# Attention heads of an encoder layer: one turned block in another PSUM bank, finer waits of the score maps, and two steps placed later

## What is computed

```python
s = q @ k.T * scale - slope * abs(qpos - kpos)     # for each of two query/key maps of 64
p = softmax(s)                                     # in fp32
w = p[map 0] - lam * p[map 1]
o = w @ v                                          # v has 128 columns
att = rms_norm(o, subln_g) * (1 - lam_init)
```

## Time and profile before

| | |
|---|---|
| time, median of 3 runs (lowest, highest) | 2149.84 us (2144.47, 2150.08) |
| the profiled execution: time, span | 2152.86 us, 2150.6 us |
| mean granted clock of TensorE in it | 0.971 |
| attention heads, sample | about 405 to 726 us |
| attention heads, prompt | about 888 to 1030 us |

### The profile page before, as it was taken

The page is one execution under the profiler, slowest core; times in us unless marked ns, Lnnn a source line. Parts: engine busy times, 40 slices in busy tenths (PEclk is TensorE's granted clock), DMA queues, the critical chain, the costliest instruction groups (busy, mean ns, idle before and its releaser), DMA issues. The chain is left out here.

```text
span 2150.6 us, 43727 instructions
## 1 busy us (share of the span) xinstructions
PE 2009.0 (93%) x16136; PEld 1760.4 (82%) x16136; DVE 1439.9 (67%) x2601; ACT 1109.6 (52%) x1983; POOL 361.3 (17%) x587
## 2 busy tenths in 40 slices
PE   7999998899998998888899399999999999999996
PEld 5887876788887776777788399999999999999895
DVE  5366466566776656766268667777777777778776
ACT  5322322466667333465222166666666666667674
POOL 1223223000000223001221101111111111111234
PEclk9999998999999999999899699999999999999998
DMA  5211100100020223212332278888878787888995
GB/s 184 85 31 32 35 27 17 44 16 24 25 65 26 67 59 90 61 49 74 118 118 99 104 255 256 254 253 256 259 249 259 252 259 248 264 270 284 331 327 188
DMA packets 183467, 317.84 MB, mean 148 GB/s; under 512 B 11872, under 2 KB 82016, under 8 KB 183328
## 3 DMA queue, kind: packets, MB, share of 16 engines
q1 hardware_dynamic: 169984, 281.06, 39.2%
q0 software_dynamic: 8608, 30.68, 5.7%
q10 hardware_dynamic: 4736, 4.19, 0.6%
HBM read 279.97 MB, written 35.91 MB: 147 GB/s over the span
## 5 line engine op out<-in xcount | busy, mean ns | idle before, releaser
L2347 DVE TENSOR_TENSOR we_lo<-raw,we_hi 128x1024 fp32r<-128x1024 f32 x384 | 466.0, 1223 | 204.7 <-ACT we_hi L2272 203.8
L2238 PE MATMUL psum<-x_parts,we_hi 128*128 128x384 f32 x2048 | 584.9, 359 | 3.3 <-DVE x_parts L2354 3.3
L2240 PE MATMUL psum<-x_parts,we_lo 128*128 128x192 f32 x2048 | 513.3, 251 | 0.0
L2272 ACT CAST we_hi<-raw 128x1024 fp32r<-128x1024 f32 x384 | 400.1, 1053 | 186.9 <-PE psum L2240 94.9
L2240 PEld LDWEIGHTS psum<-x_parts,we_lo 128*128 128x128 f32 x2048 | 392.0, 191 | 0.6
L2238 PEld LDWEIGHTS psum<-x_parts,we_hi 128*128 128x128 f32 x2048 | 385.2, 188 | 4.1 <-DVE x_parts L2354 3.6
L613 PE MATMUL psum<-hT_hi,w_hi 128*128 128x512 f32 x512 | 214.8, 420 | 0.9 <-issue 0.9
L615 PE MATMUL psum<-hT_hi,w_lo 128*128 128x512 f32 x512 | 202.0, 395 | 0.0
L614 PE MATMUL psum<-hT_lo,w_hi 128*128 128x512 f32 x512 | 201.6, 394 | 0.0
L134 POOL TENSOR_TENSOR carried_pool<-minus_half 128x1 f32<-128x1 f32 x47 | 15.8, 337 | 634.5 <-ACT result_s L2314 490.1
L615 PEld LDWEIGHTS psum<-hT_hi,w_lo 128*128 128x128 f32 x512 | 97.2, 190 | 21.9
(11 more groups left out here) (331 smaller groups left out, 4000.3 us busy)
## 6 DMA issues: line engine op xcount, KB each, us to landing
raw<-in_w_gate SPq DMA_DIRECT2D x128, 512.0 KB, 4.7
raw<-in_w_up SPq DMA_DIRECT2D x128, 512.0 KB, 6.6
raw<-in_w_down SPq DMA_DIRECT2D x128, 512.0 KB, 5.0
w_raw<-in_w_in SPq DMA_DIRECT2D x96, 256.0 KB, 2.8
y_rows<-x SPq DMA_DIRECT2D x12, 512.0 KB, 2.6
h_rows<-h SPq DMA_DIRECT2D x12, 512.0 KB, 2.9
y<-y_rows SPq DMA_DIRECT2D x12, 512.0 KB, 7.4
w_raw_s<-in_w_in SPq DMA_DIRECT2D x16, 256.0 KB, 3.0
```

Of the source, the lines that this page charges most:

```text
L2238: pe.matmul(out[:, 0:2 * SLOTS], w_hi[:, s, at], x_parts[p][:, k, :, :], start=(k == 0), stop=False, skip_group_check=True)
L2240: mm = pe.matmul(out[:, SLOTS:2 * SLOTS], w_lo[:, s, at], x_hi[p][:, k, :], start=False, stop=(k == DT - 1), skip_group_check=True)
L2272: act.copy(w_hi[:, n % PARTS, :], raw[:, s, :]).then_inc(hi.sem, 1)
L2347: dve.tensor_tensor(w_lo[:, n % PARTS, :], raw[:, n % RAW, :], w_hi[:, n % PARTS, :].bitcast(F32), ALU.subtract).then_inc(lo.sem, 1)
```

## The change

1. The sample's `("turn", 0, 1)` goes to the bank OUT; it waits for the last copy of v_rows instead of the copy of `("turn", 0, 0)`.
2. A score map waits for the takings of its own m; `taken` is raised after the queries of m = 0 and after those of m = 1, no longer after the keys.
3. In the prompt, `("take", 1)` stands behind the norm instead of in block t = 4.
4. Row quarter 2 moves from behind exp (1, 0) to behind weigh 0, quarter 3 from behind weigh 0 to behind exp (1, 1).

```diff
@@ -719,7 +719,7 @@
         joined[1][at:at] = [("o", s) for s in of]
     any_of_a = lambda step: step[0] == "a"
     unpacked = [("u", step) for step in u_p.stages[0]]
-    at_step = {("scores", 0, 0): [("h", ("split", 0))], ("exp", 1, 0): unpacked[2:3], ("weigh", 0): unpacked[3:4]}
+    at_step = {("scores", 0, 0): [("h", ("split", 0))], ("weigh", 0): unpacked[2:3], ("exp", 1, 1): unpacked[3:4]}
     in_lone = {("norm", 1): [step for _, step in unpacked[0:2]]}
     crossing = []
     for step in a_s.stages[3]:
@@ -1376,10 +1376,12 @@
         elif NB == 2:
             slots += [("take", 1), ("pieces", NT + 1)]
         else:
-            slots += [("take", 1)] * (t == NT) + [("piece", CUTS * NT + t - NT + 1)]
+            slots.append(("piece", CUTS * NT + t - NT + 1))
         if t:
             slots.append(("out", t - 1))
     slots += [(kind, NB - 1) for kind in ("squares", "mean", "norm")]
+    if NB == 1:
+        slots.append(("take", 1))
     slots += [("pieces", n) for n in range(NT + NB, last)] + [("mix", NB - 1)]
     alone = [s for s in slots if s[0] not in ("pieces", "piece", "take")]
     first = [("pieces", n) for n in range(last)]
@@ -1393,11 +1395,11 @@
 
     def apart(step):
 
-        return step[0] == "turn" and step[2] == 1 and step[1] >= NT - 2
+        return step[0] == "turn" and step[2] == 1 and (step[1] >= NT - 2 or step[1] == 0)
 
     def bank_of(step):
 
-        if step == ("v_rows", 1):
+        if step in (("v_rows", 1), ("turn", 0, 1)):
             return OUT
         return banks[0] if apart(step) else TURN
 
@@ -1458,7 +1460,7 @@
                 mm.then_inc(v_turned.sem, 1)
             elif kind == "scores":
                 t, m = step[1:]
-                pe.wait_ge(taken.sem, taken.at(i, 1))
+                pe.wait_ge(taken.sem, taken.at(i, m))
 
                 pe.wait_ge(biased.sem, biased.at(i, 2 * (t - 3 + NB) + m))
                 for b, bank in enumerate(score_banks(t, m)):
@@ -1471,6 +1473,8 @@
                 pe.wait_ge(weighed.sem, weighed.at(i, t))
                 if not apart(step):
                     pe.wait_ge(*turn_uses.before(i, step))
+                elif t == 0:
+                    pe.wait_ge(v_rows.sem, v_rows.last(i))
                 elif t == NT - 2:
                     pe.wait_ge(biased.sem, biased.last(i))
                 else:
@@ -1580,15 +1584,14 @@
                         dve.wait_ge(k_first.sem, k_first.at(j, of))
                         made = dve.tensor_tensor(k_both[of][rows_of(1 - of), 0:T], mem.land[K][rows_of(of), 0:T],
                                                 k_both[of][rows_of(of), 0:T].bitcast(F32), ALU.subtract)
-                    made.then_inc(taken.sem, 1)
                 dve.wait_ge(q_first.sem, q_first.at(j, m))
                 for half in range(2):
                     made = dve.scalar_tensor_tensor(q_lo[m][rows_of(half), 0:T], mem.land[Q][rows_of(m), 0:T],
                                                    slope_cols[rows_of(m), 0, bass.ds(j, 1)],
                                                    q_hi[m][rows_of(m), 0:T].bitcast(F32), ALU.mult, ALU.subtract)
+                made.then_inc(taken.sem, 1)
                 if m == 0:
                     return
-                made.then_inc(taken.sem, 1)
                 dve.tensor_copy(slope_now, slope_cols[:, 1, bass.ds(j, 1)]).then_inc(slopes.sem, 1)
                 dve.wait_ge(slopes.sem, slopes.at(j, 0))
             elif kind == "scores":
```

## The result

| | median (lowest to highest) | median of before, same chip | ratio, 95% interval |
|---|---|---|---|
| changed kernel | 2138.12 us (2136.48 to 2139.42) | 2149.84 | 0.994 (0.9929 to 0.9951) |
| `after_again` | 2140.58 (2137.52 to 2142.26) | 2151.33 | 0.9957 (0.9941 to 0.9973) |
| `after_third` | 2141.58 (2139.74 to 2143.37) | 2150.95 | 0.9955 (0.9942 to 0.9968) |

The change gains 9.4 to 11.7 us by medians, where 7.6 was forecast: the sign and the range (2137.5 to 2147.5) held, and the gain came out a quarter to a half larger than forecast.

The account below looks back on a forecast made before the run. TensorE, busy 2009.0 of 2150.6 us, was taken as the bound, so only closing its gaps counts. Gains 4.2 + 0.9 + 0.9 + 1.6 = 7.6 us against the median 2149.84 gave 2142.2 us, range 2137.5 to 2147.5.

Parts of the forecast that it names:

- Part 1: Sample heads: turn (0, 1) into OUT no longer waits for ScalarE's copy; three heads gain 1.40 each, 4.2 us.
- Part 2: First sample head: a score map waits only for its own queries; gain 0.9 us, 0 in the other heads.
- Part 4: Three prompt head transitions, second taking behind the norm: -1.8, +0.2 and 0, sum -1.6 us; VectorE no earlier.
- Part 3: Last sample head, row quarters later: second unit starts 2.5 us earlier, a clock fall costs 1.6, so gain 0.9.
- The first: Last sample head: no clock fall behind the 3.0 wait, TensorE keeps the 2.5; gain 9.2, 2140.6 us; chance 0.20.
- The second: Prompt transitions: the clock falls all the same; gain 5.8 or 4.2, 2144.0 to 2145.6 us; chance 0.20.
- The third: Sample heads: the bank gives nothing because ScalarE's copies hold the pace; gain 3.4, 2146.4 us; chance 0.07.
- the fourth: All attention heads: VectorE holds the pace, closed gaps come back; 5.0 slower, 2154.8 us; chance 0.03.

Follow-up runs that it names:

- after_again: The changed kernel, unedited, measured and profiled once more: 2140.58 us against 2151.33 for the kernel before, ratio 0.9957.
- after_third: The changed kernel, unedited, measured and profiled a third time: 2141.58 us against 2150.95 for the kernel before, ratio 0.9955.
- only_bank: The kernel before with only the sample's turn (0, 1) moved to the bank OUT, with its wait: 2145.9 us beside 2151.33, ratio 0.9978.
- only_rows: The kernel before with only row quarters 2 and 3 moved later: ratio 0.9996 (0.9985 to 1.0007).

## Why the prediction was right or wrong

Two terms of the sum failed, and both are falls of the clock: the last sample head (0.9 forecast, 2.5 by the means of the profiles) and the output projection (0 forecast, 1.1). The waits themselves came out nearly as replayed.

- **Part 1, the bank.** Right in kind; 1.5 to 1.6 a head instead of 1.40, 0.5 to 0.6 in all. The difference is in how the wait is counted: from the end of the matmul before. Without the wait the next one starts before that end (turn at 427.75, where the matmul before it runs from 427.51 for 0.39), so a gap that closes gives back that overlap of 0.15 too.
- **Part 2, own queries.** Right for the first sample head, 0.9. "In the other heads ... 0" is wrong for the prompt once the third edit stands: there the edit shortens a wait from 0.9 to 1.0 down to 0.3 to 0.4 at each transition. Part 4 reckoned with the short ones ("gaps of 0.5 and 0.3").
- **Part 3, the last head.** The replay was right row by row (3.0 expected, 2.88 found; the fall behind it too). What failed is the sentence that the fall after the 3.42 wait "cost nothing since the 2.00 wait followed". That was so in the one profile, where the low clock was over early; in six others of the same order it cost 0.9 to 3.1. Against their mean (1.2) the changed order (-1.3) gives 2.5 instead of 0.9, a term missed by 1.6. The decomposition was wrong too: with the bank edit in place, no gain of moving the quarters shows.
- **Part 4, the prompt.** The sum (-1.6) and each transition (-1.7, +0.1, -0.05) came out in the changed kernel. But the -1.7 is a fall of the clock, and the third edit alone avoided it in one of three profiles only, and with the second edit (and the bank) beside it in seven of seven.
- **Left out.** The fall before the output projection, 1.6. Part 4 put this place at 0 by the wait alone. The fall was in the first profile (granted clock 0.83, 0.50 and 0.81 from 992 to 998 us) and stood in no term. It came in one of three profiles of the changed kernel and in one of all seven that have the bank, own-queries and prompt edits, and in all eleven others.
- **The sum.** 0.9 + 4.8 + 1.6 came in every profile of the changed kernel, 2.5 for the last head and 1.1 (two of three times 1.6) for the output projection make 10.9, beside measured gains of 11.7, 10.75 and 9.4. The 14.6 between the two first profiles has another 4.4 from 0 to 406 and 691 to 720 us that no edit touches: luck. So is 850 to 904, which went either way by 3 in both kernels. The forecast's agreement in range is no proof of its terms: 4.2 + 0.9 + 1.6 of it held, and two places priced from one profile were 2.7 short.
- **Rivals.** The first (no fall behind the 3.0 wait) did not come in any of the three profiles, nor in the three others with this wait of 2.9. The second (falls in the transitions all the same) did not come in the changed kernel, though it does with the third edit alone. The third fell with `only_bank`, and so did the fourth, as far as it speaks of the sample; in the prompt VectorE's first map was indeed no earlier, and what was gained there was the fall alone.
- **Open.** Why the falls at the first transition and before the output projection go with the edits together and stay with any alone. The waits in front of them differ, as the table shows, and the second edit is one cause of that. This makes scattered waiting before the last wait the likely account, but it isn't shown: the pair of the second and third edits was not run, nor the changed kernel without the second. Against a rule of waits alone stands the second transition, where a wait of 2.2 was not followed by a fall in any of the eight profiles that have it. All profiles of the last row have the bank edit too; `only_bank` has the same waits here as before, so it doesn't act through these.

| edits in the prompt | waits at the first transition | fall there | waits before the output projection | fall there |
|---|---|---|---|---|
| without the third | 2.2 to 2.3 | 7 of 8 | 2.0, then 2.6 (1.9 in `only_rows`) | 8 of 8 |
| the third without the second | 0.9, 1.0 | 2 of 3 | 0.9, 0.9, then 2.6 | 3 of 3 |
| both | 0.9, 0.3, 0.3 | 0 of 7 | 0.9, 0.4, 0.3, then 2.6 | 1 of 7 |

## What to carry to other kernels

A gap that closes is worth its row, and a little more (1.5 to 1.6 for 1.40 here), since dense matmuls overlap; the queues replayed gave the waits of this change to 0.2 us. Two edits that touch the same wait are not a sum: the third makes a wait that the second shortens. What a fall of TensorE's clock costs must not be read from one profile: profile the unchanged kernel two or three times first and price each place by the mean. Where late work stands in two engines' lists, move only the engine's part that is in the way: splitting quarter 3's step between ScalarE and VectorE gave 3 us at its place beyond moving it whole. The whole program didn't keep it: 1 us by medians, which the intervals do not separate.

## What the runs showed of the hardware

- The same order and nearly the same waits (3.4, then 2.00 and 2.44) gave a low clock for one stretch in one execution and through three stretches of 4 us in another (0.60, 0.50, 0.62), 3.05 us apart.
- What a fall cost hung on the work that lay in it: nothing where it ended before the second unit (first profile), 1.6 where dense matmuls ran in it (691 to 720 us, and before the output projection).
- A wait of the same length before the output projection (2.64) was followed by a fall in both profiles of before and in one of three of the changed kernel. So the length of the last wait alone does not decide.
